# Hybrid decoder step on one core: the page work of the running sequences is issued ahead of the projection pieces in TensorE's slot

## What is computed

```python
def stick_breaking_weights(z, mask):
    log_keep = jnp.where(mask, jax.nn.log_sigmoid(-z), 0.0)
    later = jnp.concatenate([log_keep[..., 1:], jnp.zeros_like(log_keep[..., :1])], axis=-1)
    tail = lax.cumsum(later, axis=z.ndim - 1, reverse=True)
    return jnp.where(mask, jnp.exp(jax.nn.log_sigmoid(z) + tail), 0.0)
...
n = rms_norm(x, g_mix)
q, k, v, xr, gr, gates = jnp.split(n @ w_in, SPLITS, axis=-1)
attn = attend(q, k, v, sb_bias.reshape(N_KV_HEADS, GROUP))   # prompt: 1040 keys; running: 16 pages of 128 and itself
...
gate_a, gate_b = jnp.split(jax.nn.sigmoid(gates), 2, axis=-1)
x = x + (gate_a * attn + gate_b * rnn) @ w_out
```

## Time and profile before

| what | value |
|---|---|
| median of three runs | 2100.93 us |
| the profiled execution's own time | 2100.63 us |
| its span, first to last instruction | 2098.9 us |
| TensorE matmuls busy | 1902.7 us, 91% |
| VectorE busy | 1217.0 us, 58% |
| ScalarE busy | 930.9 us, 44% |
| mean granted TensorE clock over the span | 0.958 |

### The profile page before, as it was taken

How to read it: one execution, slowest core, us unless ns; L and a number is a source line. 1 busy time by engine, 2 the same in 40 slices (tenths; PEclk the granted TensorE clock), 3 DMA queues, 4 the chain that set the end, 5 groups by cost and what they waited for, 6 DMA issues and landing times. The chain is left out here.

```text
span 2098.9 us, 40932 instructions
## 1 busy us (share of the span) xinstructions
PE 1902.7 (91%) x14580; PEld 1739.5 (83%) x14580; DVE 1217.0 (58%) x1991; ACT 930.9 (44%) x1506; POOL 222.5 (11%) x106
## 2 busy tenths in 40 slices
PE   6998999899897989798995996999999999999985
PEld 5897878688786878687883776999999999999984
DVE  6101667567584858577677333655665566546645
ACT  5112676666767676667666211312222122221213
POOL 0121000000000000000003002311221122212210
PEclk9999999999998999999898997999999999999998
DMA  3334222131313232231312311211110111111104
GB/s 130 113 83 115 75 72 74 51 98 40 93 42 103 57 79 67 79 80 40 84 44 101 103 72 49 61 41 40 50 60 30 43 57 50 43 37 50 50 10 178
DMA packets 198716, 143.82 MB, mean 69 GB/s; under 512 B 58289, under 2 KB 187890, under 8 KB 198528
## 3 DMA queue, kind: packets, MB, share of 16 engines
q1 hardware_dynamic: 198554, 141.73, 23.0%
HBM read 124.31 MB, written 17.61 MB: 68 GB/s over the span
## 5 line engine op out<-in xcount | busy, mean ns | idle before, releaser
L87 PE MATMUL d_p_up<-n_hi,d_w_hi 128*128 128x346 f32 x1056 | 342.2, 324 | 15.9 <-ACT d_up L1808 8.3
L87 PE MATMUL d_p_up<-n_hi,d_w_lo 128*128 128x346 f32 x1056 | 341.6, 323 | 0.0
L87 PE MATMUL d_p_up<-n_lo,d_w_hi 128*128 128x346 f32 x1056 | 341.3, 323 | 0.0
L1911 DVE TENSOR_TENSOR mix<-mix,d_p_down 128x346 f32<-128x346 f32 x264 | 136.2, 516 | 267.7 <-PE d_p_down L1960 267.7
L87 PE MATMUL b_p_proj<-n_hi,b_w_hi 128*128 128x350 f32 x768 | 267.8, 349 | 6.8 <-ACT r_gr L1045 6.8
L87 PE MATMUL b_p_proj<-n_lo,b_w_hi 128*128 128x350 f32 x768 | 254.1, 331 | 0.0
L87 PE MATMUL b_p_proj<-n_hi,b_w_lo 128*128 128x350 f32 x768 | 253.4, 330 | 0.0
L1808 ACT ACTIVATE d_up<-d_p_up 128x346 f32<-128x346 f32 x132 | 60.2, 458 | 401.4 <-PE d_p_up L87 401.4
L87 PEld LDWEIGHTS d_p_up<-n_hi,d_w_hi 128*128 128x128 f32 x1056 | 200.7, 190 | 17.2 <-ACT d_up L1808 9.1
L87 PEld LDWEIGHTS d_p_up<-n_lo,d_w_hi 128*128 128x128 f32 x1056 | 201.1, 190 | 0.0
L87 PEld LDWEIGHTS d_p_up<-n_hi,d_w_lo 128*128 128x128 f32 x1056 | 200.8, 190 | 0.0
(11 more groups left out here) (262 smaller groups left out, 3872.1 us busy)
## 6 DMA issues: line engine op xcount, KB each, us to landing
w_raw<-in_w_in SPq DMA_DIRECT2D x45, 512.0 KB, 4.7
w_raw<-in_w_up SPq DMA_DIRECT2D x45, 512.0 KB, 3.8
b_page<-in_cache_k SPq DMA_DIRECT2D x128, 128.0 KB, 2.1
b_page<-in_cache_v SPq DMA_DIRECT2D x128, 128.0 KB, 2.1
w_raw<-in_w_down SPq DMA_DIRECT2D x22, 512.0 KB, 3.2
b_q_in<-q_scr SPq DMA_DIRECT2D x272, 32.0 KB, 2.2
mix<-in_x_prompt SPq DMA_DIRECT2D x8, 512.0 KB, 7.5
w_raw<-in_w_out SPq DMA_DIRECT2D x8, 512.0 KB, 3.2
```

The source lines that it names most:

```text
L87: last = pe.matmul(out, w[:, k, :], x[:, k, col:col + width], start=(k == 0 and w is w_hi and x is x_hi), stop=(k == KT - 1 and w is w_lo))
L1911: dve.tensor_tensor(to, to, p_down[:, n % 4, 0:FW], ALU.add).then_inc(down_out, 1)
```

## The change

In TensorE's `slots` the call of `decode` moves from behind the projection pieces, the gate chunk and the third group of turned weights to just ahead of them, behind the first two groups of turned weights. Nothing else changes, on no engine.

```diff
                         for n in range(min(groups, 2)):
                             turn(i, v, n)
+                        decode(i, s, first)
                         for piece in PLACES[s]:
                             project_piece(i, *piece)
                         if s in GATE_AT:
                             project_piece(i, GATE_AT[s], 0, KT)
                         for n in range(2, groups):
                             turn(i, v, n)
-                        decode(i, s, first)
                         if s + 1 < SLOTS:
                             scores(i, s + 1)
```

## The result

The changed kernel takes 2171.77 us (2169.71 to 2175.71, median of three runs) against 2100.93 us: 1.0347 of the time before, interval 1.032 to 1.0374. The forecast was 2166 us in a range of 2125 to 2204. The profiled execution took 2169.71 us, 69.1 more than the one before, at a mean granted clock of 0.951 against 0.958.

What follows compares the result with a forecast made beforehand. TensorE, busy 91% of the span, was taken to set the pace in slots 2 to 9. Stalls of 60 us, less 19 coming back, plus 24 for clock falls, add 65 to 2100.63: 2166 us, range 2125 to 2204.

Steps and rivals of the forecast that it cites:

- the key products: Slots 2, 4, 6, 8: TensorE waits 2.7, 1.4, 1.2, 1.6 us a turn for ScalarE's key copy, behind the score passes.
- Slot 12: Sum along the pages waits for VectorE's scan, 1.1 + 0.2 = 1.3 us a turn.
- Slot 15: TensorE waits for the first page loads, which can't move up fully: 0.65 us a turn, ends 0 and 1.5.
- Slots 3, 5 and 7: Short blocks: key-copy stalls of 0.2 us a turn for the three together, ends 0 and 1.1.
- Slots 8 to 11: Slot 8's 1.6 us stall is hidden by the 1.9 us of waits in slots 10 and 11: nothing lost.
- The clock: TensorE's granted clock falls twice more a turn, in slot 2 and among slots 3 to 6: 24 us, ends 0 and 60.
- The rival without new falls: Mixing phase: stalls come but TensorE's clock does not fall anew, 2142 us; chance 0.27.
- The turn's head: SyncE's chain starts earlier; fresh-key wait falls from 21.1 to about 11 us, floored by TensorE's loop jump: gain 10.
- The page waits: Value-page waits (5.9 us) go largely; with those for shifted values (2.4) and a clock fall, 9 us come back.
- Absorbed at the head: Rival: TensorE's delay uses up waits at the head and in slots 10 and 11, 2102 us; chance 0.05.
- faster: Rival: SyncE's chain at the turn's head decides and, with no stalls, 19 us come back, 2082 us; chance 0.05.
- Five falls a turn: Rival, slower still: TensorE's clock falls five times a turn, 2202 us; chance 0.08.

## Why the prediction was right, and where it was not

**What bounds the kernel, and the key products: right.** The copy's end less the turned weights' end, read off the old timelines, gave the new waits: slot 4 said 1.4 and measured 1.25 in nearly every turn, slot 6 1.2 and 1.09, slot 8 1.6 and 1.45, slot 2 2.7 and between 1.07 and 3.57, 20.8 us in eight turns against 21.6. (In slot 4 the copy ends at 848.37 and the products start at 848.42: the hop there is 0.05 us where 0.2 was put.) About 50 us in some 30 waits was said; 51.3 in 33 came. One reading was loose: the head's three waits are 57 of the 83 us of waiting in the earlier trace rows, two thirds, not "nearly all". That slot 2's lateness doesn't move with TensorE was right too: it hangs on VectorE (the 3.12 us in the fence on ScalarE).

**Slot 12: right**, 1.3 said, 10.1 us in 8 waits. **Slot 15: nearly**, 5.2 said for eight turns, 6.5 measured. TensorE's matmuls show hardly 0.2 us of waiting there; the wait for pages is seen on the weight loads (PEld), some 3 us in eight turns. Timeline of the changed kernel, TensorE's weight loads, slot 15 of turn 5:

```profile
920.20 0.20 PEld L1374 LDWEIGHTS b_p_kt<-b_page,b_zd 128*32 128x32 f32 x4 [0.51 <-DMA b_page<-in_cache_v]
```

The eight products, split by this wait, take 1.38 us where they took 0.67.

**Slots 3, 5 and 7: undersized**, 4.5 for 1.6 us. Only turn 0 waited in slot 3; in slot 5 the slot is 0.3 to 0.4 us longer with a wait of at most 0.1.

**Slots 8 to 11: right in kind, wrong in size.** Slots 10 and 11 did give up their waits (16.7 us less there), but slot 8 cost 16.6 us instead of 12.8, and slot 9 another 6.0, a wait of 0.69 us for VectorE's copy of the block's output in five turns. Net +5.8 where nothing was said.

**A term left out: draining.** Where no clock fall comes in, a slot grows by more than its wait: slot 6 by 1.3 for 1.09, slot 8 by 1.7 for 1.45, slot 4 by 1.5 in turn 7 for 1.25. Part of it shows in the key products, which take 0.95 us in the earlier trace rows and 1.06 in the same slot now. That matmuls overlapped across the seam and no longer do is the likely reason; no run separates it. It is about 0.25 us for each new wait, some 12 us for the 50 of them (an estimate), and a little comes without any wait: slot 14 is 0.19 us longer in every turn.

**The clock: right in the middle of the turn, overlooked at its head.** Two new falls a turn at 1.5 us were said, 16 in all and 24 us. In slots 2 to 8 the granted clock went to 0.50 seventeen times (75 us) where it had gone twice (10 us), so fifteen new ones; slot 2 grew by over 1 us beyond its wait in seven turns of eight. In slots 16, 0 and 1 it went there 8 times (38 us) where it had 12 times (72 us), and that was not in the prediction. Over the mixing phase this makes 25 stretches (113 us) after 14 (82 us). The price shows where the same slot comes with and without a fall. Windows of the changed kernel, slot 6 of turns 1 and 2, scores' end to scores' end (stretch; busy of PE, PEld, DVE, ACT, POOL; granted clock; DMA share, GB/s):

```profile
363.11:370.54 7.43, 6.34 (x74) 5.67 (x75) 4.96 (x11) 5.50 (x7) 0.00 (x0) 1.00 0.28 76
487.33:496.29 8.96, 7.87 (x73) 7.21 (x75) 4.94 (x11) 5.50 (x7) 0.00 (x0) 0.81 0.34 92
```

1.53 us more at 0.81, with TensorE idle 1.09 in both. In slot 2 the falls cost more, 1.4 to 3.0 us beyond wait and draining. The rival without new falls (2142) is out by that.

**The turn's head: the step that failed.** The prediction let the wait for fresh keys fall to 11 us and no further, since "the wait can't fall below TensorE's own jump to the loop's head". It fell to 4.9, "issue" itself from 11.0 to 3.6, the wait for slot 0's copy from 24.8 to 19.4: 29 us where 10 were said. The jump is not shorter. Source view of line 1458 in the changed kernel (duration in ns, least, median and most; first and last start), beside the earlier trace rows:

```profile
L1458 PEldq COMPARE_BRANCH  x7: 83/3753/3842, 429.5 to 1176.1; - x7
```

What changed is when it starts. The end of turn 2, where no fresh keys are awaited, shows it in both kernels: source view of line 1458 and TensorE's timeline, the kernel before first.

```profile
L1458 PEldq COMPARE_BRANCH  x1: 3882/3882/3882, 525.7 to 525.7; - x1
524.97 1.25 PE L1374 MATMUL b_p_kt<-b_page,b_zd 128*32 128x256 f32 x8
530.04 1.48 PE L1313 MATMUL b_p_z<-b_k_in,b_q_in 64*64 64x360 f32 x8 [3.81 <-issue]
...
L1458 PEldq COMPARE_BRANCH  x1: 3753/3753/3753, 554.6 to 554.6; - x1
556.85 0.75 PE L1426 MATMUL b_p_proj<-r_xc,b_gate_w 128*128 128x350 f32 x2
558.86 0.83 PE L1313 MATMUL b_p_z<-b_k_in,b_q_in 64*64 64x360 f32 x8 [1.26 <-issue]
```

In the kernel before, a turn's list ends in value products, and the branch begins about half a microsecond ahead of the last product's end (526.2). In the changed kernel it ends in projection pieces that wait for nothing, TensorE's sequencer runs ahead of the matmuls, and the branch begins 3.0 us ahead of the last piece's end (557.6). It is the same at the other ends of turns. Most of the jump lies beside the pieces, and 1.0 to 1.3 us are left; with slot 16 alone early, where the branch begins 4.0 to 5.4 us ahead, 0.1 or less is left (in both kernels in the turns without fresh keys). The Trainium skill's Runtime: NRT & Kernel Launch, section Instruction fetch mechanics, has a taken branch whose target is not among the fetched pages fetch it first. The trace's 3.3 to 3.9 us for a taken branch and 0.08 for the last, which is not taken, fit that; that the time is a fetch no run here shows. The mistake was to take a time on the sequencer for a time on the path. The floor that the prediction should have named is ScalarE's chain with the gates, 12.2 us from the last piece to slot 1's scores. Of the 31.0 us of the row of slot 16, 26.6 are shorter waits (keys 16.2, "issue" 7.4, value pages 2.4, queries 0.6); the clock, at 0.50 there for 21 us before and for none after, accounts for most of the rest.

**The page waits: wrong in sign.** They were to go largely; value pages went from 5.9 to 9.7 us (5.6 of it in slot 16 before, nearly all in slot 0 now) and 4.2 came for key pages in slot 1. The shifted values did go (2.4 to 0.3), but not by the loads that start earlier: with the value products alone early they wait 4.9 us, with the key work alone early 0.2, so that it is TensorE's delay that hides them. That both the use and the release come sooner leaves the time for a load as it was in the middle of a turn, but not near the head; which of SyncE's issues stands in the way there was not tried.

**The rivals.** Absorbed at the head (2102) and faster (2082) are out as results, but both mechanisms are there: the heads did absorb 29 us, since ScalarE's waits for VectorE's gate, which the prediction let move with TensorE, had been slack and went; and with the value products alone early the kernel is at 2082, the figure of the second. Five falls a turn (2202) is out.

## What to carry to other kernels

Before a step is moved ahead of a burst that waits for nothing, read on the other engines when its inputs are ready: the burst is the cover, and each slot loses what the producer ends behind the new place, here some 0.25 us of draining and, now and then, a clock fall. Test such a move by parts: the same edit loses 82 us in nine slots and gains 17 in four others. End a loop's body with work that waits for nothing, so that the jump lies beside it, and look for the chain that comes next (here ScalarE's gates).

## What the runs showed of the hardware

A taken loop branch of 3.3 to 3.9 us on TensorE's sequencer cost the matmuls 3.3 to 3.9 us when it started about half a microsecond ahead of the last one's end, 1.0 to 1.3 us when it started 3.0 us ahead, and 0.1 us or less when it started 4.0 us or more ahead (turns without fresh keys). A spell at the 1.2 GHz level (granted clock 0.50) cost slot 6 1.5 us. Idle stretches of 0.6 to 3.6 us between small products were followed by one in some turns and not in others, in the same slot with the same wait (slot 6: turns 2, 4 and 7 of eight, at 1.09 us). What decides between those turns stays open.
